# Projecting the forgetting heads' values for all four rounds at once

## What is computed

```python
def rms_norm(x, g):
    xf = x.astype(jnp.float32)
    y = xf * lax.rsqrt(jnp.mean(xf * xf, axis=-1, keepdims=True) + EPS)
    return (y * g.astype(jnp.float32)).astype(x.dtype)

def odd_mixer(xn, w_in, w_out, forget_b, sinks, rope_h):
    qc, kc, vc, fc, qd, kd, vd = _split(xn @ w_in, ODD_SPLITS)
    log_f = jax.nn.log_sigmoid(fc.astype(jnp.float32) + forget_b.astype(jnp.float32))
    yc = forgetting_attention(heads(qc, C_HEADS), heads(kc, C_HEADS), heads(vc, C_HEADS), log_f)
    ...
    return y @ w_out

def forgetting_attention(q, k, v, log_f):
    ...
        logits = (jnp.einsum('bqhd,bshd->bhqs', qb, k).astype(jnp.float32) * scale
                  + fq[..., None] - f_cum[:, :, None, :])
        logits = jnp.where(causal, logits, NEG)
        p = jax.nn.softmax(logits, axis=-1).astype(v.dtype)
        return jnp.einsum('bhqs,bshd->bqhd', p, v)
```

## Time and profile before

| what | value |
|---|---|
| median of 3 runs | 1775.9 us (1775.83 to 1776.26) |
| span of the profiled execution | 1773.9 us |
| TensorE busy | 1754.4 us, 99% |
| pass 0 of the stage up to the first scores | until 1227.57 us |
| scores of pass 1, 2, 3, 4 begin | 1227.57, 1245.96, 1269.78, 1293.61 us |

### The profile page before, as it was taken

One profiled execution on the slowest core, in us unless ns is written; L12 is line 12 of the kernel. 1 busy time (PEld: TensorE's weight loads), 2 busy tenths in 40 slices (PEclk: granted clock), 3 DMA queues, 4 the chain that ended last, 5 costly groups with the idle time before them and its releaser, 6 DMA issues.

```text
span 1773.9 us, 24189 instructions
## 1 busy us (share of the span) xinstructions
PE 1754.4 (99%) x8478; PEld 1423.7 (80%) x8478; DVE 1074.5 (61%) x1978; ACT 931.5 (53%) x1597; POOL 611.1 (34%) x342
## 2 busy tenths in 40 slices
PE   8999999999999999999999999999999999999998
PEld 5888768888888777778888888887778888888887
DVE  6777658999998799755455553224345655555113
ACT  6676565888886455554444443224565544444221
POOL 2333134111111322333444444444431444444442
PEclk9999999999999999999999999999999999999999
DMA  8422347999996222332233333334421333333332
GB/s 313 144 82 71 112 171 251 380 392 385 386 375 267 85 72 85 96 93 82 86 99 102 95 96 97 93 99 137 134 72 37 107 96 96 101 101 93 98 97 69
DMA packets 71480, 259.35 MB, mean 146 GB/s; under 512 B 13643, under 2 KB 18891, under 8 KB 58968
## 3 DMA queue, kind: packets, MB, share of 16 engines
q1 hardware_dynamic: 66744, 250.76, 41.5%
q0 software_dynamic: 4640, 7.32, 1.1%
HBM read 247.57 MB, written 18.43 MB: 150 GB/s over the span
## 4 chain that ended last, share of the span: by engine, by line
PE 60%; DVE 5%; issue 0%; POOL 0%; DMA 0%; SPq 0%; ACT 0%; DVEq 0%
PE ps L215 18%; PE ps L217 18%; PE ps L216 18%; DVE selb L1371 2%; DVE m L1370 1%; PE ps L569 1%; PE ps L608 1%; PE ps L597 1%; DVE prob L800 1%; DVE prob L815 1%; PE ps L583 0%; PE ps L616 0%; DVE selb L1348 0%; PE ps L631 0%; PE ps L359 0%
## 5 line engine op out<-in xcount | busy, mean ns | idle before, releaser
L282 POOL TENSOR_TENSOR ring_wl<-ring_w,ring_wh 128x1024 fp32r<-128x1024 f32 (+1 forms) x223 | 527.9, 2369 | 877.2 <-ACT ring_wh L274 771.0
L215 PE MATMUL ps<-two_x_high,ring_wh 128*128 128x512 f32 x1064 | 418.7, 394 | 1.1 <-DVE nmax L800 0.6
L216 PE MATMUL ps<-two_x_low,ring_wh 128*128 128x512 f32 x1064 | 414.2, 389 | 0.0
L217 PE MATMUL ps<-two_x_high,ring_wl 128*128 128x512 f32 x1064 | 414.2, 389 | 0.0
L274 ACT CAST ring_wh<-ring_w 128x1024 fp32r<-128x1024 f32 (+1 forms) x228 | 236.0, 1036 | 225.3 <-PE ps L217 215.3
L215 PEld LDWEIGHTS ps<-two_x_high,ring_wh 128*128 128x128 f32 x1064 | 199.7, 188 | 48.5 <-issue 4.2
L216 PEld LDWEIGHTS ps<-two_x_low,ring_wh 128*128 128x128 f32 x1064 | 199.8, 188 | 41.8 <-issue 1.2
L217 PEld LDWEIGHTS ps<-two_x_high,ring_wl 128*128 128x128 f32 x1064 | 199.7, 188 | 41.9
L1127 ACT ACTIVATE acc<-ps,param 128x512 f32<-128x512 f32 x88 | 68.6, 780 | 171.7 <-DVE ps L1147 171.7
L215 PE MATMUL ps<-hid_high,ring_wh 128*128 128x512 f32 (+1 forms) x374 | 141.0, 377 | 0.0
L216 PE MATMUL ps<-hid_low,ring_wh 128*128 128x512 f32 (+1 forms) x374 | 140.8, 377 | 0.0
(11 more groups left out here) (361 smaller groups left out, 3230.2 us busy)
## 6 DMA issues: line engine op xcount, KB each, us to landing
ring_w<-in_w_ff_up SPq DMA_DIRECT2D x88, 512.0 KB, 3.6
one_wg<-in_w_gate SPq DMA_DIRECT2D x32, 1024.0 KB
one_wu<-in_w_up SPq DMA_DIRECT2D x32, 1024.0 KB, 7.6
one_wd<-in_w_down SPq DMA_DIRECT2D x32, 1024.0 KB, 8.5
ring_w<-in_w_ff_down SPq DMA_DIRECT2D x32, 448.0 KB, 3.3
ring_w<-in_w_da SPq DMA_DIRECT2D x23, 512.0 KB, 3.6
ring_w<-in_w_ff_down SPq DMA_DIRECT2D x16, 512.0 KB, 3.5
ring_w<-in_w_rel SPq DMA_DIRECT2D x12, 512.0 KB, 4.1
```

The lines of the kernel that those rows point to most:

```text
L215: mm(out, wh, xh, start=start, stop=False)
L216: mm(out, wh, xl, start=False, stop=False)
L217: return mm(out, wl, xh, start=False, stop=stop)
L282: eng.tensor_tensor(self.low[s][:, 0:k, :], self.slab[s][:, 0:k, :], self.high[s][:, 0:k, :].bitcast(F32), ALU.subtract).then_inc(self.spl ...
```

## The change

The four v jobs of the forgetting rounds are replaced by four jobs that each hold 256 input features of the v weights of all four rounds (512 value features). All four are used in pass 0, in `joint_values`: a block of 128 tokens of `x` is the stationary operand, 512 weight columns are the moving one, and the four token blocks accumulate in banks 0, 1, 3 and 6. The result has tokens on partitions, so ScalarE writes it into `v` with four scaled copies (line 810 of the kernel after), and `turn_v`, the copy `vT` and the 128-column copies are gone for rounds 0 to 3. The ring now has six jobs in round 0 and two in each of rounds 1 to 3, twelve together as before. TensorE waits for these copies (`v_ok`) ahead of the first scores.

```diff
+JOINT = ("forget",)
+V_BANKS = (0, 1, 3, 6)
...
     def parts(self, r):
+        if self.joint(r):
+            return tuple(range(6)) if r % 4 == 0 else (0, 1)
         return (0,) if self.shared(r) else (0, 1, 2)
...
     def sync(self, sp, before_bias=None):
+        for i in self.parts(0)[3:]:
+            self.ring.load(sp, self.job(0, i))
         for r in range(1, 9):
             for i in self.parts(r):
                 self.swap(sp, self.job(r, i))
...
-                if i == 2:
+                if i == (self.parts(r)[-1] if self.joint(r) else 2):
                     mask(r)
                 ring.rest(pool, self.job(r, i) + 3)
...
+        def joint_values(r):
+
+            for a in range(4):
+                i = self.job(r, 2 + a)
+                w = [t[:, :, :].rearrange("p (k q) e -> p k (q e)", k=2) for t in ring.parts(pe, i)]
+                for k in range(2):
+                    for tt in range(TT):
+                        at = slice(P * tt, P * tt + P)
+                        mm = c.product(c.bank(V_BANKS[tt]), [t[:, 2 * a + k, at] for t in x], [t[:, k, :] for t in w],
+                                       a == 0 and k == 0, a == 3 and k == 1)
+                ring.done(mm, i)
...
+                if r == 1 and self.joint(0):
+                    pe.wait_ge(self.v_ok, 1)
                 pe.wait_ge(self.q_ok, r)
...
-            if kv:
-                emit_wait(pe, self.v_ok, r)
+            if r == 0 and self.joint(r):
+                joint_values(r)
+            if self.own_v(r):
+                emit_wait(pe, self.v_ok, self.vs(r))
...
-            if kv:
+            if self.own_v(r):
                 turn_v(r)
...
-            if kv:
+            if self.own_v(r):
                 ring.wait_used(act, self.job(r, 2))
                 nc.scalar.copy(vT[:, :], c.bank(6)).then_inc(self.v_copied, 1)
-            if r == 0:
+            if r == 0 and self.joint(0):
+                for i in range(2, 5):
+                    ring.round(act, self.job(0, i) + 3)
+                ring.wait_used(act, self.job(0, 5))
+                act.wait_ge(self.norms.col_ok, self.nth + 1)
+                at = FIRST[self.kind(0)]
+                v = buf["v"][:, at:at + 4, :].rearrange("p r (j e) -> p r j e", j=TT)
+                for tt in range(TT):
+                    ins = nc.scalar.activation(v[:, :, tt, :], c.bank(V_BANKS[tt]).rearrange("p (r e) -> p r e", r=4),
+                                               ACT.Identity, bias=c.zero[:, 0:1], scale=self.norms.col[:, tt:tt + 1])
+                ins.then_inc(self.v_ok, 1)
+                ring.round(act, self.job(0, 5) + 3)
...
-                           ("a1", heads(a["w_fgt"]) + [a["w_snk"][i] for i in (0, 4, 5, 1, 2, 3)]),
+                           ("a1", joint(a["w_fgt"], a["w_fgt_v"]) + [a["w_snk"][i] for i in (0, 4, 5, 1, 2, 3)]),
```

More of the change, by code:

```diff
@@ L422, in shared, with joint, own_v, turns @@
         return r < 8 and self.kind(r) == "sink" and r % 4 > 0
+    def joint(self, r):
+        return r < 8 and self.kind(r) in JOINT
+    def own_v(self, r):
+        return r < 8 and not self.shared(r) and not self.joint(r)
     def parts(self, r):
+        if self.joint(r):
+            return tuple(range(6)) if r % 4 == 0 else (0, 1)
         return (0,) if self.shared(r) else (0, 1, 2)
+    def turns(self, r):
+        return sum(self.own_v(n) for n in range(r))
+    def vs(self, r):
+        return sum(self.own_v(n) or (self.joint(n) and n % 4 == 0) for n in range(r))
     def kv(self, r):
@@ L600, in values @@
         def values(r, kind):
-            pe.wait_ge(self.v_ok, self.kv(r))
+            pe.wait_ge(self.v_ok, self.vs(r))
             v = self.value(r - 1)
@@ L626, in fill @@
             ring.multiply(pe, self.o0 + m, c.bank(4 + m), o, [(j, j) for j in some], start, False)
+        def joint_values(r):
[8 more added lines that the diff above has]
+                ring.done(mm, i)
         def turn_v(r):
-            pe.wait_ge(self.v_copied, r + 1)
+            pe.wait_ge(self.v_copied, self.turns(r) + 1)
             for j in range(TT):
@@ L689, in tensor @@
             if not go:
-                pe.wait_ge(self.v_ok, self.kv(8))
+                pe.wait_ge(self.v_ok, self.vs(8))
             if ka == "sink":
@@ L761, in scalar @@
                 copy_turned(r, ka, 0)
-            if kv:
+            if self.own_v(r):
                 ring.wait_used(act, self.job(r, 2))
                 nc.scalar.copy(vT[:, :], c.bank(6)).then_inc(self.v_copied, 1)
-            if r == 0:
+            if r == 0 and self.joint(0):
[10 more added lines that the diff above has]
+                ring.round(act, self.job(0, 5) + 3)
+            elif r == 0:
                 ring.round(act, self.job(0, 2) + 3)
-                if last:
-                    last(act)
+            if r == 0 and last:
+                last(act)
             if ka == "sink":
@@ L774, in scalar @@
                 ring.round(act, self.job(r, 0) + 3)
-            if kv:
-                act.wait_ge(self.v_turned, r + 1)
+            if self.own_v(r):
+                act.wait_ge(self.v_turned, self.turns(r) + 1)
                 if r == 0:
@@ L3056, in heads, with joint @@
         def heads(w, n=4):
-            return [w[r, i] for r in range(n) for i in range(3)]
+            return [w[r, i] for r in range(n) for i in range(w.shape[1])]
+        def joint(w, v):
+            return [w[0, 0], w[0, 1], *chunks(v, 4), *(w[r, i] for r in range(1, 4) for i in range(2))]
         def thirds(w):
@@ L3098, in mv, with qkv @@
         return np.ascontiguousarray(w.reshape(k // P, P, m).transpose(1, 0, 2))
-    def qkv(q, k, v):
-        return np.ascontiguousarray(np.stack([fm(q), fm(k), fm(v)], axis=1))
+    def qkv(*parts):
+        return np.ascontiguousarray(np.stack([fm(w) for w in parts], axis=1))
     def by_group(w):
@@ L3149, in pack @@
         "w_even_out": fm(i["even_w_out_2"][0]),
-        "w_fgt": qkv(wo[:, 0:512], wo[:, 512:1024], wo[:, 1024:1536]),
+        "w_fgt": qkv(wo[:, 0:512], wo[:, 512:1024]),
+        "w_fgt_v": np.ascontiguousarray(wo[:, 1024:1536].reshape(4, 2, P, 4, P).transpose(0, 2, 1, 3, 4)).reshape(4, P, DC, P),
         "w_forget": mv(wo[:, 1536:1544]),
```

## The result

The kernel after takes **1786.63 us** in the median of 5 runs (1786.39 to 1788.36), the kernel before 1775.9 in the 5 runs beside it (1775.32 to 1777.39). The ratio is 1.0062 with a 95% interval of 1.0051 to 1.0072: slower by 10.7 us, 2.0 less than forecast and within the range. The profiled execution of the kernel after has a span of 1784.5 us, 10.6 above that of before.

The account below looks back on a forecast made before the run. TensorE, busy 99% of the span, was taken to bound the kernel. -0.4 (pass 0) + 8.1 + 3.3 - 0.4 + 2.1 (clock) = +12.7 us, giving 1788.6 us; range 1783.5 to 1793.5.

Parts of the forecast that it names:

- no fall of the clock: Rival: both stalls, in passes 1 and 2, run at full clock speed; +10.6 us, 1786.5; chance 0.17.
- Pass 0, -0.4: Pass 0: `turn_v` leaves TensorE's list, about 0.4 us gained; the moved v matmuls cost nothing extra in sum.
- the bank changes cost: Rival, v matmuls in pass 0: bank changes cost +0.3 us, or +22 at half clock; 0.07 together with anything else.
- Pass 1, the stall: Pass 1: copies of the probabilities wait for job 10's cast, its load behind the second bias; TensorE idles 8.7 us, +8.1.
- The landing: Pass 1: job 10's ring load lands 12.3 us after the bias was issued, 16.7 after the first scores.
- The clock, 2.1: Behind the idle gap, expected in pass 1: TensorE's clock falls to 1.2 GHz once, costing 2.1 us.
- Pass 2, +3.3: Pass 2: job 12's load stands behind the third bias, its cast ahead of the copies; TensorE idles 3.9 us, +3.3.
- Pass 3, -0.4: Pass 3: job 14's load stands ahead of the last bias, so no stall; 0.4 us gained.
- Not slower: Rival: ScalarE's cast never waits for job 10, whose load lands quickly or passes the bias; -1.6 us, 1774.3; chance 0.06.
- Only pass 1 stalls: Rival: job 12 lands before k is used, so pass 2 gives -0.4; total +9.0 us, 1784.9; chance 0.10.
- Second fall: Rival: the clock falls in pass 2 as well; +14.8 us, 1790.7; chance 0.18.

Follow-up runs that it names:

- nine products: Kernel after with 9 idle matmuls, read by nobody, behind `turn_both` in pass 1 to fill TensorE's gap: 1787.3 us, ratio 1.006.
- four products: Kernel after with 4 idle matmuls behind `turn_both` in pass 1, leaving part of TensorE's gap idle: 1786.5 us in one run.
- narrow bias: Kernel after with the bias loads of rounds 1 to 3 cut to 32 columns a piece, same transfers and rows: 1786.64 us, ratio 1.0057.
- the kernel before with the late load: Kernel before with only the loads of jobs 7 and 8 moved behind the second bias load on SyncE: 1779.87 us, ratio 1.0021.

## Why the prediction was right

**The bound and the chain.** That TensorE was full, and that only work leaving its list or idleness entering it could move the time, held: the account, which adds up to the whole difference, is made of distances in TensorE's list alone. The chain (`shift`, bias, ring load, cast, copies, values) is the chain of waits of the kernel after, row for row, and was cut at either end with the loss gone.

**The sum.** The total came out 2.0 us below the forecast: 0.3 of it in pass 1, 0.8 in the clock and 1.6 in pass 2, against which stand the 0.5 of spread ahead of the stage and small differences. That the measured 1786.6 is the very figure of the rival *no fall of the clock* (1786.5) is chance: the clock did fall, and pass 2 lost less than that rival has.

**Pass 0, -0.4.** Measured -0.46. The v matmuls that change bank after three run at 0.227 us from start to start:

```profile
1216.68 0.39 PE L215 MATMUL ps<-ring_wh,two_x_high 128*128 128x512 f32 x1
1216.90 0.39 PE L216 MATMUL ps<-ring_wl,two_x_high 128*128 128x512 f32 x1
1217.13 0.39 PE L217 MATMUL ps<-ring_wh,two_x_low 128*128 128x512 f32 x1
1217.36 0.39 PE L215 MATMUL ps<-ring_wh,two_x_high 128*128 128x512 f32 x1
```

The last row is the first in the next bank, 0.23 behind the one ahead of it, as the earlier trace rows had it. So the rival "the bank changes cost" is out. What the Trainium skill tells of cycling through banks ("TensorE: Matmul & The Clock Gate", A second HAM failure mode: psum-queue depth-cycling) does not show here. The four scaled copies took 2.79 us (2.7 assumed) from 1238.64 and were over before the scores at 1243.97. The first bias was issued 8.6 us later than before and not 6 (1224.80 for 1216.21), and still its mask was done at 1240.12: `shift` of pass 1 waited only for the scores.

**Pass 1, the stall.** Counted from the scores: `shift` after 1.31 us (1.0 assumed), the bias after 4.71 (4.4), the cast after 16.29 (16.7), the values after 18.45 (18.8). The landing was 11.6 us after the bias was issued where I took 12.3. Without the longer values, the pass lost 9.14 - 1.33 = 7.8 us for 8.1.

**The clock, 2.1.** The mechanism was right and the size too large: 1.33 us (3.64 - 2.31 from values to scores). I took the price from the start of the span, where the engine had never worked and where, over those slow matmuls, the granted clock reads 1.00, so that they show no fall by it at all. The other falls of this study cost, in the values, 1.14 (nine products, pass 2; some 0.5 more in what follows), 1.69 (four products) and 2.16 (narrow bias, 1262.31 to 1266.78), so 2.1 was one end of what occurs.

**Pass 2, +3.3.** The term that was mis-sized most: +1.72. TensorE reached `turn_both` 13.39 us after the scores (13.37 assumed), but the cast started after 15.63 and not 17.3. 0.3 of that is an earlier `shift`, the rest the landing, 10.9 us after the bias for 12.3. I had two landings of before, of 12.3 and 12.6, and read them as a fixed time. The second was poor evidence for it: that load was issued only 8.2 us after the bias and took 4.4 from there, and with two ring loads behind the bias the amount of data was not the same either. Over these kernels the time from the bias's issue to the cast was 11.6 and 10.9 in the kernel after, 10.6 in the kernel before with the late load, and 12.3 in pass 2 with nine products. In the run where it took 12.3 pass 2 came out at 22.67 - 18.38 = +4.3, with a fall of the clock in it. So the forecast of pass 2 lay inside a spread that I should have given as one. Why it spreads stays open.

**Pass 3, -0.4.** Measured -0.29: `turn_both` to scores takes 4.72 us where it was 5.01. The cast ahead of the copies takes back a little more of `turn_v` than I allowed.

**The rivals.** *Not slower* was ruled out: in no kernel did the load pass the bias, and the cast waited 8.98 us for it. *No fall* is out by the granted clock. *Only pass 1 stalls* is out in this profile but not by much, since 2 us less would have hidden pass 2; with 256 rows of bias it is what happens. *Second fall* didn't happen in the profiled execution and did in that of another kernel.

**The reason behind the landing** was incomplete. I wrote of "the same amount of data" ahead of the load and so took the time from the right rows for the wrong cause. With the bytes as cause, narrower bias pieces would have been the remedy, and they save only 1.5 of 11.6 us in the landing and nothing in the median.

## What to carry to other kernels

When work that hides a wait is taken out of a loop, go through the strict lists of the other engines one item at a time and ask what each instruction ahead of the critical copies now waits for. Here a smaller number of ring jobs per round moved the lookahead from job 7 to job 10, past a bias load, and the kernel lost 10.7 us where the removed transposes could give about 1.5. Behind a load of many rows of 2 KB or less count the rows before the bytes, and put a load that is needed soon ahead of it.

## What the runs showed of the chip

- A load issued on the same queue behind 1024 rows of bias is ready 10.1 us after the bias was issued even with rows of 128 bytes, with the DMA engines at 0.11 and 19 GB/s; behind 256 rows it is 5.8 to 5.9. That is at least 5.5 ns a row, and 1.5 us from ten times the bytes.
- The granted clock stayed at 1.00 through idle pieces of 2.06 us (after, pass 2) and 2.46 us (four products, pass 2), and fell to 0.50 with pieces of 3.46 us (nine products, pass 2), 4.52 (four products), 6.40 (narrow bias) and 7.92 us (after). Behind the 3.46 us it fell only when TensorE was at work again.
- A fall cost 1.1 to 2.2 us in the same 16 matmuls of the values.
- A VectorE normalisation of four tiles took 3.22 us instead of 1.08 with a GpSimd subtraction of 2.50 us beside it.
- The time from a bias's issue to a cast behind it spread by over 1 us between profiles, one of each kernel, that load a full bias (10.6 to 12.3 us).
